# Behind a layer's last dot, the gathered v rows take turns over fourteen slots instead of eight

## The reference

```
def blk(xb):                                   # 128 tokens
    ...
    expert = jnp.take_along_axis(cand_idx, pos, axis=-1)
    g = jax.nn.softmax(top, axis=-1).astype(xb.dtype)
    u = jnp.take(u_tab, expert, axis=0)
    v = jnp.take(v_tab, expert, axis=0)
    a = jax.nn.gelu(jnp.einsum('td,thkd->thk', xb, u), approximate=False) * g
    return jnp.einsum('thk,thkd->td', a, v)
```

## Time and profile before

| what | us |
|---|---|
| median of three runs | 4911.98 |
| lowest and highest | 4904.36, 4916.51 |
| span of the profiled execution, first to last instruction | 4906.9 |
| PE busy | 3386.2 |
| POOL busy | 2787.7 |
| DVE busy | 2773.3 |

### The profile page before, as it was taken

How to read it: one execution, slowest core, us unless ns; L and a number is a source line. 1 busy time by engine, 2 the same in 40 slices (tenths; PEclk the granted TensorE clock), 3 DMA queues, 4 the chain that set the end, 5 groups by cost and what they waited for, 6 DMA issues and landing times.

```text
span 4906.9 us, 48457 instructions
## 1 busy us (share of the span) xinstructions
PE 3386.2 (69%) x15780; PEld 1734.7 (35%) x15780; DVE 2773.3 (57%) x7116; ACT 840.3 (17%) x1947; POOL 2787.7 (57%) x2575
## 2 busy tenths in 40 slices
PE   7778787985667896647765679567789655644433
PEld 4544335442324443324332443343453322211110
DVE  1136666546665656546666663147565666766662
ACT  1112212221211212102211120121121211111100
POOL 0005666446656757656667765115565767777775
PEclk8978888897788898768876879778879877866665
DMA  5759999889999999999999999349989999999997
GB/s 207 257 179 357 405 383 390 317 310 404 342 361 384 363 399 385 409 409 368 400 375 400 410 388 384 124 167 347 382 334 403 380 406 403 408 401 398 404 406 299
DMA packets 502171, 1747.60 MB, mean 356 GB/s; under 512 B 55072, under 2 KB 75808, under 8 KB 501664
## 3 DMA queue, kind: packets, MB, share of 16 engines
q0 software_dynamic: 368640, 1342.34, 70.5%
q1 hardware_dynamic: 115616, 389.05, 20.7%
q10 hardware_dynamic: 17664, 13.11, 0.8%
HBM read 1729.08 MB, written 15.20 MB: 355 GB/s over the span
## 4 chain that ended last, share of the span: by engine, by line
PE 37%; DMA 28%; issue 12%; POOL 9%; DVE 9%; ACT 4%; SPq 0%; POOLq 0%; DVEq 0%; ACTq 0%
PE ps L762 34%; DMA vr<-in_v_tab,idxT 19%; DMA ur<-in_u_tab,idx 5%; POOL ur L724 5%; POOL vr L735 5%; PE ps L765 3%; DVE ur L1783 2%; DMA wring<-in_w_mod 1%; DVE mx L1660 1%; ACT arena L1330 1%; DMA wring<-in_w_gb 1%; DMA wring<-in_w_pq 1%; ACT arena L1333 1%; DVE mx L1658 1%; ACT arena L1235 1%
## 5 line engine op out<-in xcount | busy, mean ns | idle before, releaser
L1783 DVE CUSTOM_DVE_ANT_0 ur<-ur,hn 128x1024 f32<-128x1024 f32 x1280 | 1562.0, 1221 | 837.9 <-DMA ur<-in_u_tab,idx 833.6
L724 POOL DMA_INDIRECT ur<-in_u_tab,idx x1280 | 1404.6, 1097 | 1084.9 <-DVE idx L1866 493.0
L735 POOL DMA_INDIRECT vr<-in_v_tab,idxT x1280 | 1379.4, 1078 | 1012.8 <-PE ps L762 483.5
L762 PE MATMUL ps<-vr,spread 128*32 128x512 f32 x5120 | 921.1, 855 | 927.2 <-DMA vr<-in_v_tab,idxT 926.7
L762 PE MATMUL ps<-wring,arena 128*128 128x512 f32 x2272 | 1054.0, 614 | 78.8 <-DMA wring<-in_w_qkv 30.4
L762 PEld LDWEIGHTS ps<-vr,spread 128*32 128x32 f32 x5120 | 186.1, 138 | 1438.2 <-issue 1437.1
L762 PEld LDWEIGHTS ps<-wring,arena 128*128 128x128 f32 x2272 | 431.4, 196 | 628.7 <-issue 564.7
L762 PE MATMUL ps<-wring,hT 128*128 128x256 f32 x1280 | 329.4, 409 | 52.2 <-DMA wring<-in_w_pq 52.1
L765 PE MATMUL ps<-ident,arena 128*128 128x128 f32 x976 | 196.6, 349 | 215.1 <-ACT arena L1333 133.7
L762 PEld LDWEIGHTS ps<-wring,hT 128*128 128x128 f32 x1280 | 258.4, 208 | 164.9 <-issue 70.8
L765 PEld LDWEIGHTS ps<-ident,arena 128*128 128x128 f32 x976 | 148.3, 178 | 309.2 <-ACT arena L1333 159.1
(11 more groups left out here) (175 smaller groups left out, 2795.4 us busy)
## 6 DMA issues: line engine op xcount, KB each, us to landing
wring<-in_w_gb SPq DMA_DIRECT2D x232, 512.0 KB, 7.0
wring<-in_w_pq SPq DMA_DIRECT2D x160, 512.0 KB, 7.6
wring<-in_w_mod SPq DMA_DIRECT2D x96, 512.0 KB, 6.9
wring<-in_w_out SPq DMA_DIRECT2D x80, 512.0 KB, 7.0
wring<-in_w_qkv SPq DMA_DIRECT2D x68, 512.0 KB, 7.2
wring<-in_w_conv SPq DMA_DIRECT2D x60, 512.0 KB, 7.5
ur<-in_u_tab,idx POOLq DMA_INDIRECT x1280, 9.1
vr<-in_v_tab,idxT POOLq DMA_INDIRECT x1280, 9.2
```

Source lines behind the costliest of these rows:

```text
L724: nc.gpsimd.indirect_dma_start(ur[:, row % UR, :], None, u_rows, bass.IndirectOffsetOnAxis(ap=idx[:, at:at + 1], axis=0)).then_inc(u_in[ro ...
L735: nc.gpsimd.indirect_dma_start(vr[:, row % VR, :], None, v_rows, bass.IndirectOffsetOnAxis(ap=idxT[:, pair % 3, i:i + 1], axis=0)).then_in ...
L762: return nc.tensor.matmul(o, lhsT, rhs, start=first, stop=last, skip_group_check=True)
L1783: v.tensor_tensor_reduce(u, u, hn[:], 1.0, 0.0, ALU.mult, ALU.add, dots[:, j % 2, k:k + 1]).then_inc(s["dots_done"], 1)
```

## The change

A function `slots` lays out a table before the program is written. For every row of u and of v it holds the ring ("u" or "v"), the slot, the number of the use of that slot and who used it before. Up to a layer's last u row all is as before: u rows go around `ur`, v rows around `vr`. From the first step without a u row on, the v rows take eight turns in `vr`, six in `ur`, eight in `vr`, and so on. A gather waits for the earlier user of its slot, be it a dot or a sum, and the consumers wait for the semaphore of the slot that the table names. Since 12 of layer 0's v rows go to `ur`, the rows of layer 1 lie in other slots of `vr` than before, in the same turn.

```
+def slots():
+
+    u_at, v_at, users = {}, {}, {}
+    turns = {"u": 0, "v": 0}
+
+    def take(ring, size, who):
+        slot = (ring, turns[ring] % size)
+        turns[ring] += 1
+        earlier = users.setdefault(slot, [])
+        earlier.append(who)
+        return slot + (len(earlier), earlier[-2] if len(earlier) > 1 else None)
+
+    for l in range(LAYERS):
+        r0, n = P * FIRST[l], P * COUNT[l]
+        for S in range(n + BEHIND):
+            if S < n:
+                u_at[r0 + S] = take("u", UR, ("dots_done", r0 + S + 1))
+            if S >= BEHIND:
+                row = r0 + S - BEHIND
+                ring = "u" if S >= n and (S - n) % (UR + VR) >= VR else "v"
+                v_at[row] = take(ring, UR if ring == "u" else VR, ("v_used", row + 1))
+    return u_at, v_at
...
+        U_AT, V_AT = slots()
+
+        def held(at):
+            ring, k, n, _ = at
+            return (ur[:, k, :], u_in[k], 16 * n) if ring == "u" else (vr[:, k, :], v_in[k], 16 * n)
+
...
             def gather_v(row):
                 pair, at = divmod(row, PAIR)
                 w.wait_ge("it_done", pair + 1)
-                w.wait_ge("v_used", row + 1 - VR)
+                before = V_AT[row][3]
+                if before:
+                    w.wait_ge(*before)
                 pool.sem_inc(s["pool_turn"], 1)
 
                 i = 8 * (at % 4) + at // 4
+                v, landed, _ = held(V_AT[row])
                 nc.gpsimd.indirect_dma_start(
-                    vr[:, row % VR, :], None, v_rows, bass.IndirectOffsetOnAxis(ap=idxT[:, pair % 3, i:i + 1], axis=0)
-                ).then_inc(v_in[row % VR], 16)
+                    v, None, v_rows, bass.IndirectOffsetOnAxis(ap=idxT[:, pair % 3, i:i + 1], axis=0)
+                ).then_inc(landed, 16)
...
                 for r in range(row, row + 4):
-                    pe.wait_ge(v_in[r % VR], 16 * (r // VR + 1))
+                    _, landed, n16 = held(V_AT[r])
+                    pe.wait_ge(landed, n16)
...
-                               vr[:, r % VR, half * BW:(half + 1) * BW], opens, True)
+                               held(V_AT[r])[0][:, half * BW:(half + 1) * BW], opens, True)
```

More of the change, by code:

```diff
@@ L720, in gather_u @@
                 w.wait_ge("idx_done", j + 1)
-                w.wait_ge("dots_done", row + 1 - UR)
+                before = U_AT[row][3]
+                if before:
+                    w.wait_ge(*before)
                 pool.sem_inc(s["pool_turn"], 1)
                 at = j % PH * TOPK + k
+                u, landed, _ = held(U_AT[row])
                 nc.gpsimd.indirect_dma_start(
-                    ur[:, row % UR, :], None, u_rows, bass.IndirectOffsetOnAxis(ap=idx[:, at:at + 1], axis=0)
-                ).then_inc(u_in[row % UR], 16)
+                    u, None, u_rows, bass.IndirectOffsetOnAxis(ap=idx[:, at:at + 1], axis=0)
+                ).then_inc(landed, 16)
             def gather_v(row):
@@ L1779, in dot @@
                 j, k = divmod(row, TOPK)
-                u = ur[:, row % UR, :]
-                dve.wait_ge(u_in[row % UR], 16 * (row // UR + 1))
+                u, landed, n16 = held(U_AT[row])
+                dve.wait_ge(landed, n16)
                 w.wait_ge("gelu_done", j - 1)
```

## The result

The changed kernel takes 4878.96 us (median of four runs, 4876.93 to 4890.53), the kernel before 4910.86 us (median of four, 4904.36 to 4916.51). The ratio is 0.9942, with a 95% interval of 0.9926 to 0.9957: 28.5 us less, 21 to 36. The forecast was 4886 us, with 4878 to 4900 as range, and "faster" with a chance of 0.84.

The account below looks back on a forecast made before the run. In each layer's last 36 steps, v gathers were taken to stall for slots that PE's sums free. Gains of 13.4 and 12.9 us, other terms 0, gave 26.3 us less: 4885.7 us, range 4878 to 4900.

Parts of the forecast that it names:

- T0 to T4 unchanged: First v gathers of each layer's last 36 steps: same slots and waits, T4 still waiting 9.86 and 5.07 us; gain nothing.
- T5 to T11, waits for the last dots at no cost: Next gathers of each tail: the last dots start over 10 us before T8 is issued, so cost 0.
- T12 to T35, fourteen slots are enough, POOL's pace is late next: Rest of each tail: 14.6 us fits into 17.4, stalls go; gains 13.4 us in layer 0, 12.9 in layer 1.
- What is late next: Both tails without stalls: POOL's issue pace of 1.243 us a row sets the time, with 0 to +2.9 us as range.
- the first rival: Both tails: transfers, not issues, set the pace, at 1.47 us a row; 4899.5 us, chance 0.06.
- The last sum: PE's last sum in each tail: +1.7 us in layer 0 at worst, -1.6 in layer 1 at best; taken as 0.
- The sum: Both tails together: 26.3 us less, span 4906.9 to 4880.6 us, time 4885.7 us.
- Only the end gains: Passage between the layers, or layer 1 behind it, takes back layer 0's 13.4 us; 4899.1 us, chance 0.06.
- It doesn't do what it says: Both tails: gathers in `ur` still end up waiting and the stalls stay; 4912 us, chance 0.03.
- Slower through the clock of the passage: Passage between the layers: PE stays at the lower clock level, 48.2 us more; 4933.9 us, chance 0.04.

Follow-up runs that it names:

- u first: Changed kernel, but both tails begin with the six slots of u, then eight of v: ratio to the kernel before 0.9949 in each of two sets.
- the two halves: Changed kernel with slots of u used only in layer 0's last 36 steps, or only in layer 1's: ratios to the kernel before 0.9969 and 0.9968.

## Why the prediction was right, point by point

- *T0 to T4 unchanged*: right. T4 waited 10.91 and 5.08 us, the 2.00 us before T5 stayed. u first showed that T4's wait is for a slot of v.
- *T5 to T11, waits for the last dots at no cost*: right, no row waits over 0.31 us.
- *T12 to T35, fourteen slots are enough, POOL's pace is late next*: the issues were right to 0.1 us, 38.48 and 37.26 against 38.53 and 37.29. That slots of v stall when they come round after ten rows and not after twelve fits the sum of 14.6 us.
- *What is late next*: this term was mis-sized. The prediction let the last sum follow T35 as before, after 6.4 to 6.6 us. It came after 8.59 and 8.29, since 31 rows at 1.243 us run ahead of transfers that need 1.28 each. (1.28 - 1.243) x 31 is 1.1 us, and the long interval adds 1.2 in layer 0 and 1.5 in layer 1. In layer 1 that is 0.9 more than the 1.7 lost, since the sum of T4 started only 5.66 us behind T7's issue there, where 6.55 were the rule. Why that interval is long is not tested; an instruction fetch starts inside it. The two tails lost 2.2 + 1.7 = 3.9 us, a little beyond the 2.9 that stood as the upper bound for the pace. It was in fact the first rival in mechanism, at under a third of its price (3.9 of 13.8 us): it put 1.47 us a row on full transfers, and they need 1.28. The prediction took full transfers to cost no more than the 2.9 us of its range, by 1.29 us a row; the long intervals were not in it.
- *The last sum*: 1.92 us in layer 0 as before, 3.64 in layer 1 in place of 3.47. Taken as 0, measured +0.2. In layer 1 the last sum took 3.64 us behind a wait of 1.41, in layer 0 1.92 us behind one of 1.43; the granted clock was 0.50 in the one and 1.00 in the other. The Trainium skill ("TensorE: Matmul & The Clock Gate", section "HAM oscillation — how this bites in real kernels") says that short bursts of matmuls with longer waits for transfers between them start at the slow clock each time. These two rows show that a short wait just ahead is not enough for the fast one.
- *The sum*: 26.3 expected; 22.3 measured from T4 (11.3 + 11.0). The interval of the ratio, 21 to 36 us, holds both. The rest of the 31.7 us between the two profiled executions is of the size of the variation and was no part of the mechanism. The profiled tails alone would give 4910.9 - 22.3 = 4888.6 us, 2.9 above the forecast of 4885.7. The median of 4879.0 is 6.7 below it and only 1 us inside the range. So the mechanism is carried by the two tails; that the median fell below the forecast and not above it is variation.
- *Only the end gains*: out, by the two halves. *It doesn't do what it says*: out. *Slower through the clock of the passage*: out, the passage did not grow: 138.8 to 144.1 us in the traces with the change, 142.2 and 139.0 in the two of the kernel before.

## What to carry to other kernels

How many buffers a gather loop needs is one sum from the trace: the issues until a consumer's group is complete, the landing, the consumer's work and the release, divided by the interval of the issues. Here 14.6 us by 1.243 us is 11.7: slots of v that came round after ten rows stalled, after twelve they did not. Redo the sum with the landing that the changed kernel will have. With the 8.4 us of the tail's end in place of 6.5 it is 16.5 us, by an estimate that no run tests 13 to 14 slots in a loop that goes on like this. When the slots are no longer short, look at once at whether the issuer then asks for more than the transfers carry: 422 GB/s asked and 410 carried moved the last landing back by some 2 us. Issuing earlier then gains only the idle time of the transfers that it fills, 6.4 us in layer 1 and 1.5 in layer 0. And where a change touches some 2% of a run, read it in its own stretch: the stretches beside it varied by as much as half of its worth.

## What the runs showed of the hardware that was not expected

- POOL issues an indirect gather of 128 rows of 4 KB every 1.243 us, and one of 64 rows every 1.198.
- On two of the chips used, POOL saw PE's counts up to 7 us behind the recorded end of the matmuls, in 23 to 38 gathers into `vr` a run, and always at T22 in a tail with fourteen slots and v first (eight traced tails, two of them with half the bytes). Those traces hold 1070 to 1095 counts of `v_used` of 1280, the others that count once for each row 1278 to 1281. All kernels took about 3% longer there. The cause is open.
- One packet of 16384 B of the instruction queue (1.03 us) starts in each tail, and seven of eight times the one long interval between sums, 5.8 to 6.6 us in place of 5.12, lies around it.
- The 2.00 us before T5 in layer 1 appear with and without the change and on both kinds of chip; with half of the bytes, with twelve slots and with u first they are missing. No run names the cause.
